# Projection products of a hybrid decoder layer, cut as 512 prompt columns + 8 sample columns instead of 256 + 264

## What is computed

```python
h = rmsnorm(x, g_mix)
proj = h @ w_in + b_in
q, k, v, o, ig, fg, u, gl = jnp.split(proj, offsets, axis=-1)
hA, C, n, m = mlstm_mixer(q, k, v, ig, lf, C0, n0, m0)      # chunkwise over the prompt, one step for samples
yA = (sigmoid(o) * hA_normed) @ w_a
yS, sr, si = s5_mixer(u, ...)                                # complex diagonal state space
yS = gelu(yS); yS = yS * sigmoid(yS @ w_glu + b_glu)
yB = yS @ w_b
gA, gB = jnp.split(gl, 2, axis=-1)
x = x + (sigmoid(gA) * yA + sigmoid(gB) * yB) @ w_out
hf = rmsnorm(x, g_ffn)
x = x + (silu(hf @ w_ff1) * (hf @ w_ff3)) @ w_ff2
# at the end a last RMSNorm; the recurrent states of both groups are outputs too
```

## Time and profile before

| | |
|---|---|
| time, median of 2 runs | 1141.4 us (1140.48 to 1142.32) |
| span of the profiled execution | 1138.9 us |
| PE busy | 1042.8 us, 92%, 8296 matmuls |
| weight loads busy | 999.0 us, 88%, 8296 loads |
| DVE busy | 622.6 us, 55% |
| ACT busy | 377.0 us, 33% |
| POOL busy | 229.4 us, 20% |
| chain that ended last | PE 73%, DVE 18%, ACT 4%, issue 3% |
| weight transfers | 147 of 512 KB |

### The profile page before, as it was taken

How to read it: one execution, slowest core, us unless ns; L and a number is a source line. 1 busy time by engine, 2 the same in 40 slices (tenths; PEclk the granted TensorE clock), 3 DMA queues, 4 the chain that set the end, 5 groups by cost and what they waited for, 6 DMA issues and landing times.

```text
span 1138.9 us, 20711 instructions
## 1 busy us (share of the span) xinstructions
PE 1042.8 (92%) x8296; PEld 999.0 (88%) x8296; DVE 622.6 (55%) x1061; ACT 377.0 (33%) x521; POOL 229.4 (20%) x327
## 2 busy tenths in 40 slices
PE   0476899999999999998999999999999999999994
PEld 0476789888998899788999999999999999999994
DVE  7999753867276747556433444654444444433333
ACT  4123231423242413346333333343333434222220
POOL 2994626180627250102000000000000000000000
PEclk9988898989789988979999999999999999999997
DMA  5113031612342133314433232222222222223211
GB/s 210 56 56 117 21 110 38 236 37 74 119 153 73 37 141 133 112 75 171 162 112 110 92 106 99 92 83 87 91 91 92 92 92 92 93 93 108 96 55 75
DMA packets 26778, 113.35 MB, mean 100 GB/s; under 512 B 3344, under 2 KB 3392, under 8 KB 24816
## 3 DMA queue, kind: packets, MB, share of 16 engines
q1 hardware_dynamic: 21744, 79.21, 20.6%
q0 software_dynamic: 3408, 29.15, 7.0%
q10 hardware_dynamic: 1584, 4.40, 1.0%
HBM read 98.84 MB, written 13.91 MB: 99 GB/s over the span
## 4 chain that ended last, share of the span: by engine, by line
PE 73%; DVE 18%; ACT 4%; issue 3%; DMA 1%; POOL 0%; DVEq 0%; ACTq 0%
PE G L1221 60%; PE Q L1375 4%; PE Q L1332 2%; PE Q L1322 2%; DVE w_low L756 1%; ACT c_samples L374 1%; PE G L1289 1%; DVE u_by_step L955 1%; PE Q L1221 1%; PE G L1356 1%; DVE s_tmp L992 1%; PE Q L1300 1%; DVE s_tmp L993 1%; DVE s_state L994 1%; DVE x_scaled L837 1%
## 5 line engine op out<-in xcount | busy, mean ns | idle before, releaser
L1221 PE MATMUL G<-h_high,w_high 128*128 128x256 f32 (+1 forms) x1424 | 299.7, 293 | 38.3 <-DVE h_low L832 19.8
L1221 PE MATMUL G<-h_low,w_high 128*128 128x256 f32 (+1 forms) x1424 | 295.5, 290 | 0.0
L1221 PE MATMUL G<-h_high,w_low 128*128 128x256 f32 (+1 forms) x1424 | 295.3, 290 | 0.0
L756 DVE TENSOR_TENSOR w_low<-raw,w_high 128x1024 fp32r<-128x1024 f32 x147 | 186.1, 1270 | 171.7 <-ACT w_high L374 171.5
L1221 PEld LDWEIGHTS G<-h_high,w_high 128*128 128x128 f32 x1424 | 230.6, 197 | 44.8 <-issue 32.7
L374 ACT ACTIVATE w_high<-raw 128x1024 fp32r<-128x1024 f32 x147 | 155.0, 1060 | 305.1 <-PE G L1221 297.9
L1221 PEld LDWEIGHTS G<-h_low,w_high 128*128 128x128 f32 x1424 | 230.1, 196 | 0.0
L1221 PEld LDWEIGHTS G<-h_high,w_low 128*128 128x128 f32 x1424 | 229.5, 195 | 0.0
L1221 PE MATMUL G<-hidden_low,w_high 128*128 128x256 f32 x352 | 71.1, 283 | 0.0
L1221 PE MATMUL G<-hidden_high,w_high 128*128 128x256 f32 x352 | 70.9, 283 | 0.0
L1221 PE MATMUL G<-hidden_high,w_low 128*128 128x256 f32 x352 | 70.7, 282 | 0.0
(11 more groups left out here) (333 smaller groups left out, 1568.8 us busy)
## 6 DMA issues: line engine op xcount, KB each, us to landing
raw<-wst SPq DMA_DIRECT2D x147, 512.0 KB, 3.3
c_samples<-c POOLq DMA_DIRECT2D x4, 2048.0 KB, 9.4
out_cs<-c_samples POOLq DMA_DIRECT2D x4, 2048.0 KB, 6.9
v_spread<-v_scratch POOLq DMA_DIRECT2D x4, 1024.0 KB, 5.1
x_tokens<-xt SPq DMA_DIRECT2D x4, 520.0 KB, 6.4
heads_scratch<-head_h POOLq DMA_DIRECT2D x4, 520.0 KB, 3.0
heads_out<-heads_scratch POOLq DMA_DIRECT2D x1, 2080.0 KB, 9.0
x_residual<-xt POOLq DMA_DIRECT2D x1, 2080.0 KB, 8.6
```

The costliest lines, as they stand in the source:

```text
L756: tt(WL[n.slot()][:], raw[n.slot()][:], WH[n.slot()][:].bitcast(F32), ALU.subtract).then_inc(w_lo, 1)
L1221: last = mm(o, w[slot][:, c], h[:, k, c0_:c0_ + width], start=start and x == 0 and t == 0, stop=stop and x == n - 1 and t == 2)
```

## The change

`HALVES` becomes ((0, 512), (512, 8)), and every place that writes or reads the two parts follows: the first bank of a pair is filled with the 512 prompt columns, the second with the 8 sample columns. The number of instructions stays the same on every engine. The core of the diff:

```diff
-HALVES = ((0, 256), (256, 264))
+HALVES = ((0, SEQ), (SEQ, NS))
...
             def tiles(pair):
                 t = G if pair < 4 else Q
-                return [t[:, pair % 4, 0:256], t[:, pair % 4 + 1, 0:264]]
+                return [t[:, pair % 4, 0:SEQ], t[:, pair % 4 + 1, 0:NS]]
...
-                tt(ff_a[0][:, 0:256], G[:, A, 0:256], fr[:, 0:256], ALU.mult)
-                tt(ff_a[0][:, 256:T], G[:, A + 1, 0:264], fr[:, 256:T], ALU.mult).then_inc(ffa_ready, 1)
+                tt(ff_a[0][:, 0:SEQ], G[:, A, 0:SEQ], fr[:, 0:SEQ], ALU.mult)
+                tt(ff_a[0][:, SEQ:T], G[:, A + 1, 0:NS], fr[:, SEQ:T], ALU.mult).then_inc(ffa_ready, 1)
...
-                    act.activation(oS[:, e, 0:256], G[:, pair, 0:256], ACT.Sigmoid, bias=curv("bias")[:, 5 + e:6 + e])
-                    act.activation(oS[:, e, 256:T], G[:, pair + 1, 0:264], ACT.Sigmoid,
+                    act.activation(oS[:, e, 0:SEQ], G[:, pair, 0:SEQ], ACT.Sigmoid, bias=curv("bias")[:, 5 + e:6 + e])
+                    act.activation(oS[:, e, SEQ:T], G[:, pair + 1, 0:NS], ACT.Sigmoid,
...
-            mm(Q[:, 2, 0:256], ones[:], facc[:, 0:256], start=True, stop=True)
-            mm(Q[:, 3, 0:264], ones[:], facc[:, 256:T], start=True, stop=True).then_inc(fsq_summed, 1)
+            mm(Q[:, 2, 0:SEQ], ones[:], facc[:, 0:SEQ], start=True, stop=True)
+            mm(Q[:, 3, 0:NS], ones[:], facc[:, SEQ:T], start=True, stop=True).then_inc(fsq_summed, 1)
```

More of the change, by code:

```diff
@@ L406, in _ @@
             act.wait_ge(sq_summed, 1)
-            act.activation(rx[:, 0:256], G[:, B, 0:256], ACT.Sqrt, bias=eps[:, 0:1], scale=1.0 / D).then_inc(rx_root, 1)
-            act.activation(rx[:, 256:T], G[:, B + 1, 0:264], ACT.Sqrt, bias=eps[:, 0:1], scale=1.0 / D).then_inc(rx_root, 1)
+            act.activation(rx[:, 0:SEQ], G[:, B, 0:SEQ], ACT.Sqrt, bias=eps[:, 0:1], scale=1.0 / D).then_inc(rx_root, 1)
+            act.activation(rx[:, SEQ:T], G[:, B + 1, 0:NS], ACT.Sqrt, bias=eps[:, 0:1], scale=1.0 / D).then_inc(rx_root, 1)
             for k in range(KC):
@@ L428, in glu @@
                 act.wait_ge(smp_done, H)
-                act.activation(sg[:, m, 0:256], G[:, pair, 0:256], ACT.Sigmoid, bias=b_glu[:, m:m + 1])
-                act.activation(sg[:, m, 256:T], G[:, pair + 1, 0:264], ACT.Sigmoid, bias=b_glu[:, m:m + 1]).then_inc(y2_raw, 1)
+                act.activation(sg[:, m, 0:SEQ], G[:, pair, 0:SEQ], ACT.Sigmoid, bias=b_glu[:, m:m + 1])
+                act.activation(sg[:, m, SEQ:T], G[:, pair + 1, 0:NS], ACT.Sigmoid, bias=b_glu[:, m:m + 1]).then_inc(y2_raw, 1)
             def head(i, n, last_head):
@@ L521, in _ @@
                     act.wait_ge(ml_ready, m.val(1, 1))
-                    act.activation(t[:, 0:256], G[:, A, 0:256], ACT.Sigmoid, bias=cur_b[:, g:g + 1])
-                    act.activation(t[:, 256:T], G[:, A + 1, 0:264], ACT.Sigmoid, bias=cur_b[:, g:g + 1]).then_inc(ready, 1)
+                    act.activation(t[:, 0:SEQ], G[:, A, 0:SEQ], ACT.Sigmoid, bias=cur_b[:, g:g + 1])
+                    act.activation(t[:, SEQ:T], G[:, A + 1, 0:NS], ACT.Sigmoid, bias=cur_b[:, g:g + 1]).then_inc(ready, 1)
                     high(n.plus(2 * g + RING))
@@ L543, in _ @@
             act.wait_ge(fsq_summed, 1)
-            act.activation(fr[:, 0:256], Q[:, 2, 0:256], ACT.Sqrt, bias=eps[:, 0:1], scale=1.0 / D)
-            act.activation(fr[:, 256:T], Q[:, 3, 0:264], ACT.Sqrt, bias=eps[:, 0:1], scale=1.0 / D).then_inc(fr_root, 1)
+            act.activation(fr[:, 0:SEQ], Q[:, 2, 0:SEQ], ACT.Sqrt, bias=eps[:, 0:1], scale=1.0 / D)
+            act.activation(fr[:, SEQ:T], Q[:, 3, 0:NS], ACT.Sqrt, bias=eps[:, 0:1], scale=1.0 / D).then_inc(fr_root, 1)
             for f, n in steps(act, F_TILES, 2, 3, N_FF):
@@ L560, in _ @@
             act.wait_ge(fsq_summed, 2)
-            act.activation(fr[:, 0:256], Q[:, 2, 0:256], ACT.Sqrt, bias=eps[:, 0:1], scale=1.0 / D)
-            act.activation(fr[:, 256:T], Q[:, 3, 0:264], ACT.Sqrt, bias=eps[:, 0:1], scale=1.0 / D).then_inc(fin_root, 1)
+            act.activation(fr[:, 0:SEQ], Q[:, 2, 0:SEQ], ACT.Sqrt, bias=eps[:, 0:1], scale=1.0 / D)
+            act.activation(fr[:, SEQ:T], Q[:, 3, 0:NS], ACT.Sqrt, bias=eps[:, 0:1], scale=1.0 / D).then_inc(fin_root, 1)
             for m in range(KC):
@@ L888, in early @@
                 for half in range(2):
-                    own.add(ts(ub[:, 32 * half:32 * half + 32, :], G[:, B + half, 0:256].rearrange("p (b t) -> p b t", t=L),
+                    own.add(ts(ub[:, 32 * half:32 * half + 32, :], G[:, B, 256 * half:256 * half + 256].rearrange("p (b t) -> p b t", t=L),
                                bias[:, 0:1], None, ALU.add))
-                ts(uT[:, SEQ:T], G[:, B + 1, 256:264], bias[:, 0:1], None, ALU.add).then_inc(u_ready, 1)
+                ts(uT[:, SEQ:T], G[:, B + 1, 0:NS], bias[:, 0:1], None, ALU.add).then_inc(u_ready, 1)
                 low(n.plus(RING))
@@ L1119, in _ @@
                     own_wait = used
-                    tt(t[:, 0:256], t[:, 0:256], G[:, B, 0:256], ALU.mult).then_inc(mrg, 1)
-                    tt(t[:, 256:T], t[:, 256:T], G[:, B + 1, 0:264], ALU.mult).then_inc(used, 1)
+                    tt(t[:, 0:SEQ], t[:, 0:SEQ], G[:, B, 0:SEQ], ALU.mult).then_inc(mrg, 1)
+                    tt(t[:, SEQ:T], t[:, SEQ:T], G[:, B + 1, 0:NS], ALU.mult).then_inc(used, 1)
                     low(n.plus(2 * g + 1 + RING))
@@ L1145, in _ @@
                 src = [(G if bank < 4 else Q)[:, (bank + h) % 4:(bank + h) % 4 + 1, 0:w] for h, (_, w) in enumerate(HALVES)]
-                tt(X1[:, mm, 0:256], X1[:, mm, 0:256], src[0], ALU.add).then_inc(x1_half, 1)
-                tt(X1[:, mm, 256:T], X1[:, mm, 256:T], src[1], ALU.add).then_inc(x1_ready, 1)
+                tt(X1[:, mm, 0:SEQ], X1[:, mm, 0:SEQ], src[0], ALU.add).then_inc(x1_half, 1)
+                tt(X1[:, mm, SEQ:T], X1[:, mm, SEQ:T], src[1], ALU.add).then_inc(x1_ready, 1)
                 dve.wait_ge(xfl_ready, m.val(1, 1))
@@ L1192, in _ @@
                 pair = A if m.static % 2 == 0 else B
-                tt(X1[:, mm, 0:256], X1[:, mm, 0:256], G[:, pair:pair + 1, 0:256], ALU.add).then_inc(x1_half, 1)
-                tt(X1[:, mm, 256:T], X1[:, mm, 256:T], G[:, pair + 1:pair + 2, 0:264], ALU.add).then_inc(x2_ready, 1)
+                tt(X1[:, mm, 0:SEQ], X1[:, mm, 0:SEQ], G[:, pair:pair + 1, 0:SEQ], ALU.add).then_inc(x1_half, 1)
+                tt(X1[:, mm, SEQ:T], X1[:, mm, SEQ:T], G[:, pair + 1:pair + 2, 0:NS], ALU.add).then_inc(x2_ready, 1)
                 dve.wait_ge(xsq2, m.val(1, 1))
@@ L1231, in _ @@
             pe.wait_ge(sq_added, KC)
-            mm(G[:, B, 0:256], ones[:], xacc[:, 0:256], start=True, stop=True)
-            mm(G[:, B + 1, 0:264], ones[:], xacc[:, 256:T], start=True, stop=True).then_inc(sq_summed, 1)
+            mm(G[:, B, 0:SEQ], ones[:], xacc[:, 0:SEQ], start=True, stop=True)
+            mm(G[:, B + 1, 0:NS], ones[:], xacc[:, SEQ:T], start=True, stop=True).then_inc(sq_summed, 1)
             unit(At(0), HH, HL, A, ready=hl_ready)
```

4 lines of the change are left out of this document (2 added, 2 removed).

## The result

The changed kernel takes 1774.55 us (1773.81 to 1775.29, 2 runs) against 1141.40 us before: 1.5547 times as long, 95% interval 1.5495 to 1.5599. The forecast had the direction but not the size; 1774.55 lies far outside 1400 to 1500.

The account below looks back on a forecast made before the run. PE's matmul pairs of line 1221 were taken as the bound: 3092 full-clock pairs add 300.5 us, 100 half-clock pairs 20.6, minus 10 absorbed, 311 us; 1138.9 + 311 + 2.5 = 1452 us, range 1400 to 1500.

Parts of the forecast that it names:

- The pair: Line 1221's wide plus narrow matmul: 337 ns at full clock (325 to 348) against 239.8, the narrow one's following load open.
- the wide one: The 512-column matmul of each line 1221 pair: 225 ns, its 213.3 ns stream plus 11.6 ns on top.
- One sign: In the new trace of line 1221: narrow start 216 to 225 ns after the wide, next wide 112 ns later.
- The count at half clock: Line 1221 pairs in 14 half-clock stretches between 73 and 537 us: about 100, each 206 ns more.
- The rival of the clock: The new pattern loses full clock everywhere, a pair costing 636 ns: 925 us more, 2377 us; chance 5%.
- The double pass: Line 1221's 8-column fp32r matmuls run in two passes, another open load per pair: 367 us more, 1819 us; chance 9%.
- Two loads ahead: The loader also takes the next wide matmul's load early, a pair costing 230 ns: 1110 us; chance 5%.
- DVE, ACT, transfers: Evacuations 0.1 us longer but hidden by the next unit, open under 1 us; weight transfers get more cover.
- The setup: First 100 us, bound by DVE's setup with PE waiting: waits absorb 10 us of slower PE (0 to 25).

Follow-up runs that it names:

- e7_wide: The changed kernel (512 + 8) without its narrow matmuls except the first of each unit, evacuations kept: 1133.20 us.
- e2_ffn: 256 + 264 columns up to the output stage, 512 + 8 only in the feed-forward and w_ff2 units: 1303.45 us.
- e10_order: The changed kernel with PE's pause before the first merge unit taken away and each step's three wide matmuls put before its three narrow ones: 1477.23 us.
- e4_nopause: The changed kernel with one ACT instruction moved, giving the first merge unit's credit after the third GLU half-unit, not the fourth: 1513.46 us.
- e8_c384: All stages cut as 384 + 136 columns instead of the changed kernel's 512 + 8: 1265.30 us.
- e5_drop: e2_ffn plus 56 one-column fp32 matmuls (results unused) after the first feed-forward round: 1786.36 us.
- e1_burst: The changed kernel plus 6 dense 512-column fp32 matmuls (12 passes, results unused) on PE after the first merge round: 1541.83 us.

## Why the prediction was wrong

**The pair.** Right, by its own steps. The load after the narrow matmul lies open. In the changed kernel itself the load row shows it:

```profile
1300.03 0.30 PEld L1221 LDWEIGHTS G<-h_high,w_low 128*128 128x128 f32 x2
1300.37 0.30 PEld L1221 LDWEIGHTS G<-h_high,w_high 128*128 128x128 f32 x2
```

Two loads of 0.19 us stand in each 0.30 us, so they follow each other after 0.11 us, and the next one comes 0.23 us later. 337 ns were forecast and 342 measured, at half clock 636 and 635 to 640. The term that was a little short is the wide one: 225 ns, and 232 measured. One sign was forecast wrongly: a narrow start 216 to 225 ns after a wide one, and the next wide start 112 ns later. The records start 315 and 27 ns apart. The sum is the same; the record of a wide matmul behind a narrow one is 0.48 us long, against 0.39 to 0.40 for one behind a wide one in e7_wide, so it seems to begin before its load is done.

**The count at half clock.** This is the step that failed: "over the 14 such stretches ... so about 100 pairs". It carried the clock's history over from the kernel before as if it were a fixed stretch of the program, and only priced the pairs in it anew. In fact 1201 pairs ran at half clock. The history is an outcome of the pattern: pauses and narrow runs of the same kind lower the clock in both kernels, but the 256 + 264 pattern brings it back in some microseconds and 512 + 8 in turn doesn't, until a dense fp32 stretch happens to come. At the prices measured, the pairs that were forecast make 3092 x 0.102 + 100 x 0.21 = 336 us, the 1101 others 327 us more, and PE waits 25 us less in all: 638 us, for 633 measured. So the miscount is half of the loss, and all but a few us of what the forecast missed.

**The rival of the clock** had the right agent and 5%, at 2377 us, for a clock lost everywhere. I looked for a pattern that pulls the clock down and found none, and that was right: e2_ffn runs 529 us of 512 + 8 at full clock. I did not ask the second question, whether the pattern lifts it again, though the trace before has every fall there was to start from. The two prices, the two levels and a way down were all in rows 2, 4 and 8. The rival that was missing, "stays down after the next fall until something dense comes", costs 0.3 us for each pair in between on top of 1452.

**The double pass** (1819 us, 9%) comes nearest to the measured time and is false: 8296 records as before, and e2_ffn at 101 ns a pair has no room for a second load. A time alone would have named the wrong cause here.

**Two loads ahead** (1110 us) is false: the load row has its gaps, 87% busy, and the pair is 342 ns. With it falls the reading of the Trainium skill's "TensorE: Matmul & The Clock Gate", section "Step-by-step: what each phase is for", in which loads run any distance ahead; one load ahead is what the load rows of the changed kernel and of e10_order show. The 131 ns of its section "Back-to-back issue gap" for 512 columns in a stream with loads don't hold for these fp32r matmuls: 232 ns between wide ones in e7_wide.

**DVE, ACT, transfers.** Right: nothing of theirs is on the path. PE's waits in the feed-forward loop are none, and the 512-wide evacuation took 0.69 us.

**The setup.** I had 10 us absorbed by waits, with 25 as the upper end, and it was the end: PE's idle time fell from 96 to 71 us (span less busy time). The 7.4 and 8.8 us waits of the earlier trace rows went away, and so did the 7.1 us for the convolution kernels, while the wait for head_h grew from 6.7 to 11.3 us. These 15 us that I took off too little, and the 5 ns a pair that I had too little at full clock (3092 x 0.005 = 15 us), are the two misses that cancel. But the pairs there run at half clock too: 34.72 us for 54 of them. The clock column is 1.00 in this stretch,

```profile
55.00:85.00 30.00, 30.00 (x95) 25.44 (x95) 1.00 0.11 36
```

while 95 matmuls in 30 us are 632 ns a pair. The clock record of this trace seems to hold nothing ahead of 140 us; the distance from start to start is what to trust there.

## What to carry to other kernels

Where every matmul loads its own weights, cut the moving columns evenly: a stream as long as the load hides it, and a narrow rest opens one whole load (here 111 ns), whatever its own width (8, 72 and 136 columns were tried). Price a new pattern at both levels of the clock, and ask of it not only whether it lowers the clock but whether it brings a lowered one back; if it doesn't, a fall of the clock is worth all the time up to the next dense stretch. Then look for what lowers it: two microseconds of waiting, or one instruction's place on ACT, decided over 261 us here (e4_nopause). Not every such pause lowers it: in the kernel before one of three did, and in e8_c384 the one of 2.05 us did not.

## What had not been expected of the hardware

- The granted clock has a memory. The same 512 + 8 pattern ran 529 us at 1.00 in e2_ffn and about 1000 us at 0.50 in e5_drop, in the same stages; 7 us of dense fp32 matmuls moved it up until the last wait of the kernel, 819 us later (e1_burst), a pause of 2.06 us down.
- 448 + 72 and 384 + 136 recover, 512 + 8 in turn doesn't, and 512 + 8 with three wide and three narrow ones in a row does (e10_order). Their prices are 313, 285 and 342 ns a pair; where between 448 and 512 it turns, and by what measure, was not tried.
- An fp32r matmul of 8 columns is a single record of 167 ns, in one pass, and costs its load (0.11 us); there is no penalty for being narrow beyond that.
- The 11.6 ns that a 260-column fp32r matmul takes above its stream at full clock grow with the width, but less than it does: 232 - 213 = 19 ns at 512. What they are was left open; at half clock there is nothing of the kind (215 ns for 260 columns).
